# Expert stages of a two-block transformer: 32 slots of 32 rows in four column groups, the two slots of each expert one behind the other

## What is computed

```python
N_EXPERTS, TOP_K, D_EXPERT = 16, 2, 512
def grouped_moe(h, w_router, router_bias, w_gate, w_up, w_down):
    t = h.reshape(-1, D)                          # 256 x 1024
    ...
    combine = (jax.nn.one_hot(eidx, N_EXPERTS, dtype=jnp.float32) * w[..., None]).sum(-2)
    for e in range(N_EXPERTS):
        he = jax.nn.silu(t @ w_gate[e]) * (t @ w_up[e])
        y = y + combine[:, e:e + 1] * (he @ w_down[e]).astype(jnp.float32)
```

## Time and profile before

| | us |
|---|---|
| median of 3 runs | 1887.92 (1886.70 to 1888.09) |
| span of the profiled execution | 1886.8 |
| PE busy | 1814.0 (96%) |
| expert blocks of layer 0 on PE, first gate and up to last down | 308.8 to 586.1 |
| the same, layer 1 | 870.6 to 1135.6 |

### The profile page before, as it was taken

One profiled execution on the slowest core, in us unless ns is written; L12 is line 12 of the kernel. 1 busy time (PEld: TensorE's weight loads), 2 busy tenths in 40 slices (PEclk: granted clock), 3 DMA queues, 4 the chain that ended last, 5 costly groups with the idle time before them and its releaser, 6 DMA issues.

```text
span 1886.8 us, 28242 instructions
## 1 busy us (share of the span) xinstructions
PE 1814.0 (96%) x11785; PEld 1285.6 (68%) x11802; DVE 753.6 (40%) x1282; ACT 663.2 (35%) x1076; POOL 74.5 (4%) x132
## 2 busy tenths in 40 slices
PE   5999999989999999999999999999899999999998
PEld 2888785323335888785333336767699999779998
DVE  4593553000004683553000005213265557656555
ACT  2325441111114335441111112141154556655443
POOL 0000001100001000001100010000000000100000
PEclk8999999999999999999999999999999999999999
DMA  9769955999986665856999957879954543444440
GB/s 377 313 268 374 350 240 236 428 427 428 428 347 273 237 273 226 340 243 245 428 428 427 416 221 288 352 309 415 399 215 182 193 159 112 139 174 179 178 178 22
DMA packets 52755, 540.89 MB, mean 287 GB/s; under 512 B 6768, under 2 KB 11248, under 8 KB 21680
## 3 DMA queue, kind: packets, MB, share of 16 engines
q1 hardware_dynamic: 42800, 505.66, 66.4%
q0 software_dynamic: 9856, 33.82, 4.7%
HBM read 589.53 MB, written 28.84 MB: 328 GB/s over the span
## 4 chain that ended last, share of the span: by engine, by line
PE 80%; DMA 9%; DVE 6%; DVEq 2%; issue 1%; ACT 1%; SPq 0%; ACTq 0%
PE bank L1375 15%; PE bank L995 10%; PE bank L997 10%; PE bank L996 10%; PE bank L1402 7%; PE bank L1045 6%; DMA ring<-in_w_up 5%; PE bank L1054 3%; PE bank L1587 3%; PE bank L1178 2%; PE bank L1506 1%; DMA ring<-in_mlp_w 1%; DMA ring<-in_lru_w_out 1%; PE bank L1353 1%; DVE small L295 1%
## 5 line engine op out<-in xcount | busy, mean ns | idle before, releaser
L995 PE MATMUL bank<-split_x,split_w 128*128 128x256 f32 x896 | 251.3, 280 | 0.8 <-DVE split_w L2828 0.8
L996 PE MATMUL bank<-split_x,split_w 128*128 128x256 f32 x896 | 250.6, 280 | 0.0
L997 PE MATMUL bank<-split_x,split_w 128*128 128x256 f32 x896 | 249.7, 279 | 0.0
L2719 DVE TENSOR_TENSOR hidden<-cqkv,bank 128x256 f32<-128x256 f32 x46 | 19.4, 421 | 515.0 <-ACT cqkv L1947 515.0
L2828 DVE TENSOR_TENSOR split_w<-ring,split_w 128x1024 fp32r<-128x1024 f32 x128 | 156.4, 1225 | 98.0 <-ACT split_w L2074 98.0
L996 PE MATMUL bank<-hx_lo,ring_lo 128*128 128x256 f32 (+1 forms) x656 | 183.6, 280 | 0.0
L995 PEld LDWEIGHTS bank<-split_x,split_w 128*128 128x128 f32 x896 | 168.4, 188 | 1.2 <-DVE split_w L2828 1.2
L996 PEld LDWEIGHTS bank<-split_x,split_w 128*128 128x128 f32 x896 | 168.7, 188 | 0.0
L997 PEld LDWEIGHTS bank<-split_x,split_w 128*128 128x128 f32 x896 | 168.7, 188 | 0.0
L2074 ACT ACTIVATE split_w<-ring 128x1024 fp32r<-128x1024 f32 x128 | 134.4, 1053 | 94.0 <-PE bank L997 87.5
L995 PE MATMUL bank<-hx_hi,ring_lo 128*128 128x256 f32 (+1 forms) x528 | 150.5, 285 | 0.0
(11 more groups left out here) (410 smaller groups left out, 2962.0 us busy)
## 6 DMA issues: line engine op xcount, KB each, us to landing
ring<-in_ada SPq DMA_DIRECT2D x48, 2048.0 KB, 11.5
ring<-in_w_gate SPq DMA_DIRECT2D x32, 2048.0 KB, 13.4
ring<-in_w_up SPq DMA_DIRECT2D x32, 2048.0 KB, 18.5
ring<-in_w_down SPq DMA_DIRECT2D x32, 2048.0 KB, 16.8
ring<-in_mlp_w SPq DMA_DIRECT2D x32, 2048.0 KB, 7.6
ring<-in_w_in SPq DMA_DIRECT2D x16, 2048.0 KB, 11.7
mix<-in_w_gate SPq DMA_DIRECT2D x14, 2048.0 KB, 15.7
mix<-in_w_up SPq DMA_DIRECT2D x14, 2048.0 KB, 20.2
```

Source lines behind the costliest of these rows:

```text
L995: pe.matmul(out, hi, x_hi, start=start, stop=False, **kw)
L996: pe.matmul(out, hi, x_lo, start=False, stop=False, **kw)
L997: return pe.matmul(out, lo, x_hi, start=False, stop=stop, **kw)
```

## The change

Blocks become **slots** of 32 rows. Every expert has 64 own rows in the buffer as before, in two slots that follow each other: slot 2e (`own`, rows 0 to 31) and slot 2e+1 (`flex`, rows 32 to 63). There are no extra blocks. Rows over 64 of an expert go in pieces of 32 rows to the flex slot of an expert that has at most 32 rows (a host; hosts are tried in the order 2, 3, ..., 15, 0, 1). Such a **guest** needs its own weights: SP loads them, under a condition, over the host's weights when the host's own slot is done with them. With the counts above layer 0 has two guests (of experts 6 and 7, in slots 5 and 7) and layer 1 has one (of expert 13, in slot 5).

In a slot the stationary operand has 32 columns, and four matmuls of 256 streamed columns go to four column groups (`32 * g`). The rows of four slots come with four transfers and one set of transposes. Results are stored in four pieces a slot. The last four slots (`KEPT`) are multiplied from SBUF, each as 8 matmuls over 32 rows of the array (`kept_results`).

```diff
-CAP = 64
-XB = (2 * T - 1) // CAP
+ROWS_OF_SLOT = 32
+OWN = 2 * ROWS_OF_SLOT
+SLOTS_OF = [(e, kind) for e in range(NE) for kind in ("own", "flex")]
+GROUPS_BEHIND = {GROUP * (q - 1) + 1: q for q in range(1, NG_ROWS)}
...
                 for n, (e, kind) in enumerate(SLOTS_OF):
+                    then = e if kind == "own" else e + BUFFERS
+                    if then < NE:
+                        which = None
+                        if kind == "own":
+                            i = GUESTS.index(e)
+                            which = (sp.value_load(flex[0:1, i:i + 1], min_val=0, max_val=NE - 1),
+                                     sp.value_load(flex[0:1, NE + i:NE + i + 1], min_val=0, max_val=1))
+                        sp.wait_ge(MP.sem, MP.at(f"gu{n}", l))
+                        load(then, 0, which)
+                        load(then, 1, which)
                     if held:
-                        load(*held)
-                    held = (n, (2,), which)
+                        sp.wait_ge(MP.sem, MP.at(f"d{held[0]}", l))
+                        load(*held[1:])
+                    held = (n, then, 2, which) if then < NE else None
...
                     for k in part:
-                        for g in range(2):
+                        for g in range(4):
                             ins = pe.matmul(
-                                banks[n % 2][CAP * g:CAP * g + CAP, :].rearrange("p (u c) -> p u c", u=2), xT[:, k, :],
-                                gu[:, :, k, 256 * g:256 * g + 256], start=(k == 0), stop=(k == KT - 1))
+                                banks[n % 2][32 * g:32 * g + 32, 0:256].rearrange("p (u c) -> p u c", u=2),
+                                xpT[n // GROUP % 2][:, k, at:at + ROWS_OF_SLOT],
+                                gu[:, :, k, P * g:P * g + P], start=(k == 0), stop=(k == KT - 1))
...
-                        for g in range(2):
-                            at = CAP * (1 - g if n == NB - 1 else g)
-                            ins = pe.matmul(banks[2 + n % 2][at:at + CAP, :],
-                                            hTs[n % 2][:, k % 2, CAP * (k // 2):CAP * (k // 2) + CAP],
-                                            wd[:, k, 512 * g:512 * g + 512], start=(k == 0), stop=(k == 3))
+                        for g in range(4):
+                            ins = pe.matmul(banks[2 + n % 2][32 * g:32 * g + 32, 0:256],
+                                            hTs[n % 2][:, 32 * k:32 * k + 32],
+                                            wd[:, k, 256 * g:256 * g + 256], start=(k == 0), stop=(k == 3))
...
+                def kept_results(n):
+                    pe.wait_ge(MA.sem, MA.at(f"out{n}", l))
+                    i = KEPT.index(n)
+                    for j in range(2):
+                        for g in range(4):
+                            rows_ = slice(32 * g, 32 * g + 32)
+                            ins = pe.matmul(y_of(2 * g + j), outs[n % OUTS][rows_, P * j:P * j + P], shareT[i // 2][rows_, i % 2, :],
+                                            start=(i == 0 and j == 0), stop=True, skip_group_check=True)
                 down(NB - 1)
+                for n in KEPT[:-1]:
+                    kept_results(n)
                 for t in range(TT):
                     earlier_results(t)
-                pe.wait_ge(MA.sem, MA.at(f"out{NB - 1}", l))
-                for k in range(KT):
-                    ins = pe.matmul(y_of(k), outs[k // 4][:, P * (k % 4):P * (k % 4) + P], shareT[:, k // 4, :],
-                                    start=False, stop=True, skip_group_check=True)
+                kept_results(NB - 1)
...
+                flex_at = {e: pool.value_load(flex[0:1, 2 * NE + i:2 * NE + i + 1], min_val=0, max_val=ROWS - ROWS_OF_SLOT)
+                           for i, e in enumerate(GUESTS)}
+                group_rows(1)
...
+                pool.wait_ge(MP.sem, MP.at(f"gu{SLOT_AT[NE - 2, 'flex']}", l))
                 for i in (0, 2, 1, 3):
```

More of the change, by code:

```diff
@@ L86, in _const @@
     for name, n in [("ident", P), ("ones", P), ("freq", 1), ("heads", P), ("turn", DQK), ("pair", 8 * P),
-                    ("future", 2 * P), ("before", P), ("own", NE), ("more", NE), ("extras", XB)]:
+                    ("future", 2 * P), ("before", P), ("own", NE), ("more", NE), ("host", NE), ("host row", NE)]:
         CONST[name] = (at, n)
@@ L382, with loads_before @@
 BUFFERS = 3
[L383 to L408, removed]
+SLOTS_OF = [(e, kind) for e in range(NE) for kind in ("own", "flex")]
+NB = len(SLOTS_OF)
+SLOT_AT = {slot: n for n, slot in enumerate(SLOTS_OF)}
+LOADS = [2 * len(range(i, NE, BUFFERS)) for i in range(BUFFERS)]
+LAST_BLOCK = [SLOT_AT[max(range(i, NE, BUFFERS)), "flex"] for i in range(BUFFERS)]
+GROUP = P // ROWS_OF_SLOT
+NG_ROWS = NB // GROUP
+OUTS = 4
+KEPT = list(range(NB - OUTS, NB))
+FIRST_UNSTORED = min(SLOTS_OF[n][0] for n in KEPT)
+GROUPS_BEHIND = {GROUP * (q - 1) + 1: q for q in range(1, NG_ROWS)}
+RAWS = [len(range(i, NG_ROWS - 1, 3)) for i in range(3)]
+WEIGHTED = [3, 4]
+def loads_before(n):
+    e, kind = SLOTS_OF[n]
+    return 2 * (e // BUFFERS) + 1 + (kind == "flex")
 def moe_steps():
@@ L2308, in places @@
             total = counts[:, TT * NE:(TT + 1) * NE]
-            more, upto, first, below = line(), line(), line(), line()
-            over, base, steps = cols(TT, NE), cols(TT, NE), cols(NE, 3)
-            tt(steps, total.unsqueeze(2).broadcast_to([P, NE, 3]), limits.unsqueeze(1).broadcast_to([P, NE, 3]), ALU.is_gt)
+            more, upto, first, below, spare, rank = line(), line(), line(), line(), line(), line()
+            which, used, guest_row = line(), line(), line()
+            over, base = cols(TT, NE), cols(TT, NE)
+            steps = krs[:, 0:NE * STEPS_OVER].rearrange("p (a b) -> p a b", b=STEPS_OVER)
+            passed = rs[:, 0, 0:NE * NE].rearrange("p (a b) -> p a b", a=NE)
+            tt(steps, total.unsqueeze(2).broadcast_to([P, NE, STEPS_OVER]),
+               limits.unsqueeze(1).broadcast_to([P, NE, STEPS_OVER]), ALU.is_gt)
+            ts(spare[:, 0:NE - 2], total[:, 2:NE], ROWS_OF_SLOT + 0.5, None, ALU.is_lt)
+            ts(spare[:, NE - 2:NE], total[:, 0:2], ROWS_OF_SLOT + 0.5, None, ALU.is_lt)
             wait()
@@ L2336, in places @@
             nc.vector.tensor_reduce(at, both, AX, ALU.add)
+            tt(flex[:, 0:NE], which, const("host"), ALU.add)
+            tt(flex[:, 2 * NE:3 * NE], guest_row, const("host row"), ALU.add)
+            tt(flex_row[:, :], guest_row, const("host row"), ALU.add)
             wait()
@@ L2981, in shape_constants @@
     e = np.arange(NE, dtype=np.float32)
-    put("own", np.tile(CAP * e, (P, 1)))
-    put("more", np.tile(CAP * (NE - 1) - CAP * e, (P, 1)))
-    put("extras", np.tile(np.arange(XB, dtype=np.float32), (P, 1)))
+    put("own", np.tile(OWN * e, (P, 1)))
+    put("more", np.tile(OWN * (NE - 1) - OWN * e, (P, 1)))
+    hosts = np.array(GUESTS, np.float32)
+    put("host", np.tile(hosts, (P, 1)))
+    put("host row", np.tile(OWN * hosts + ROWS_OF_SLOT, (P, 1)))
     return con
```

313 lines of the change are left out of this document (156 added, 157 removed).

## The result

The changed kernel takes 1946.24 us (median of 4 runs, 1941.32 to 1949.38), against 1888.01 us (4 runs, 1886.70 to 1892.45) for the kernel before on the same chip. The ratio is 1.0303, with a 95% interval from 1.0281 to 1.0325. The profiled execution has a span of 1941.7 us, 54.9 us over that of before. The forecast was 1875.

What follows compares the result with a forecast made beforehand. Expert stages have two nearly equal lines, transfers (240 us) and PE (277 us); unchanged transfers limit the gain. -8.1 - 12.7 + 2 x 3.7 = -13.4 us on 1886.8 gives 1873.4 span, median 1.1 over: 1875 us, range 1861 to 1895.

Steps and rivals of the forecast that it cites:

- PE's part: Expert stages: small matmul instructions step at 0.055 us, so a slot takes 5.43 us and an expert 11.5 us.
- the two additions: Before each layer's last `down`: 0.9 us for slower instructions after a wait, 1.5 us for gathers during the last expert's loading.
- The second rival: PE's small-instruction step stays at 0.07 to 0.08 us, a slot takes 7.8 us, in all 1948 us; chance 0.10.
- The volume: Expert stages still load 15 and 14 experts; layer 0's weights, token rows and results take 238 us at 425 GB/s.
- The fourth rival: Transfers lose more through 1 KB stores, four times the requests and longer guest gaps: 1909 us, half of it 1892; chance 0.15.
- The third, gaps at guests: Reason in the rival of slower transfers: the weights' queue has longer gaps at guests than the 9.4 and 7.4 us counted.
- Covered edits: Edits taken as hidden: `shares` some 1.7 us behind slots 3 and 4 each, POOL's four transfers a slot 2.7 us of 8.
- 16.8 us for three guests: Weights' queue empty 9.4 us in layer 0 and 7.4 in layer 1, because requests wait for guests' slots and downs.
- The kept slots: End of each stage: 64 matmuls over 32 array rows at 0.115 us each, 7.4 us, +3.7 in each layer.
- the first rival: Row groups run side by side, and neither slower clock nor gathers cost anything: 1862 us; chance 0.17.
- The new `places` ... +2.0 us: DVE chain from counts to one-hot matrix, ahead of the expert stage: a dozen more operations, +2.0 us, all on the path.

Runs made afterwards that it cites:

- the rows early: Changed kernel, but POOL reads two hosts' row numbers before requesting the first token rows and the other fourteen afterwards: 1927.36 us, ratio 1.0220 to the kernel before.
- the strided kernels: Changed kernel with each of four token-row transfers filling every fourth partition; ratios to the kernel before: 1.0042 (early, from third set), 1.0045 (early, all sets), 1.0180 (late, all sets).

## Why the prediction was wrong

**PE's part was right.** 0.055 us a step, so 5.4 us a slot. The last `down` came 12.1 us behind the last weights (599.4 to 611.5), forecast 12.0 with the two additions. The second rival named 1948 us, near what was measured, but its mechanism is refuted by that step: a right number for a wrong reason, by luck. (The 12 us that it adds besides 28 and 20 have no working either.)

**The volume was right, the rate was not.** "Layer 0: 94.4 + 3.7 + 3.7 MB ... is 238 us at 425 GB/s" took the rate of a kernel whose token rows came over 128 partitions for one with 32. The last byte was forecast 247.5 us after the start of the queue and came after 281.8. The narrow transfers cost 23 us in both layers together (1.0303 against 1.0180, rows late in both), or 33 with the rows early (1.0220 against 1.0045). With rows late and one transfer of 128 from the third set on it is 15 (1.0222); whether the other 8 lie in the first set or in the spread between series of runs is not shown. The fourth rival put 17 us on each layer, where 12 to 17 were found, but of its reasons the runs refute two: with 1 KB stores and four requests a slot all in place, the strided kernels have 425 GB/s and packets of 613 or 614 ns from 443 to 520 us. The third, gaps at guests, holds in cost.

**The failed step.** "Covered edits: ... POOL issues four transfers a slot at 0.53 us each". This counts POOL's transfers and not the 16 reads ahead of them, in front of the first rows that PE needs: 16 x 0.57 = 9.1 of the 13.05 us, the other 3.9 being there with two reads as well. The diff shows the loop of value loads directly ahead of `group_rows(1)`; no number for such a read stood in the sum, and with it no hole of 13 us in each layer's queue. It cost 26 us. The second step that failed is the 425 GB/s of the paragraph above, 23 us.

**Guests.** "The queue runs dry only because expert e+3 can be asked for when the guest's slot is done": the mechanism was right and dips are where they were expected (379, 418 and 438 us, later than forecast by the hole), and their lengths nearly so: 2.1 + 3.5 + 5.2 = 10.8 us in layer 0 and 2.4 + 5.3 = 7.7 in layer 1 with rows early and strided, forecast 9.4 and 7.4. But 16.8 us for three guests were 26, 9 more. A gap costs more than its own length: counted in bytes against 425 GB/s, the first three cost 17.9 us and the other two 12.2.

**Smaller terms.** The kept slots cost 0.3 us more than before (3.96 for 3.62) and not 3.7: four row groups run side by side, as the first rival had it; 7 us of the forecast were too much. "The new `places` ... +2.0 us" was 2.9 in layer 0, read from the last count matmul to the first gate and up (10.3 us before, 13.2 after). The end of the stage has 1.07 us of waiting for ACT behind the kept slots that was not foreseen.

**The balance.** From 1875 to 1946 are 71 us. 26 are the late rows, 23 the narrow transfers, 9 the guests' gaps beyond the forecast, by the runs without guests. 13 more are left: the kernel without late or narrow transfers takes 1896 us where 1875 + 9 = 1884 would be expected. By its trace, the last `down` of layer 0 comes 11.8 us later than forecast, that of layer 1 another 13.0, and the rest of the kernel is 2.6 us faster (a sum of 22, these 9 and 13). Most of it stands in the two queues: from first to last byte they take 259.1 and 239.6 us, forecast 247.5 and 230.6, so 20.6 us more. Of these 13 are the gaps at guests as counted in bytes, 5 are lost at the queues' start and end, and 2 are volume. So the guests' part may be 13 and not 9. None of this remainder was tested by an edit of its own.

## What to carry to other kernels

A transfer that shares its time with a full queue is priced by what it does to the queue's packets, and that goes by the partitions it fills: beside transfers to 32 or 64 neighbouring ones the others took 7 to 36% longer (656 to 834 ns for 614, in the windows from 333 to 346 and from 443 to 520 us), beside 32 in steps of four 613 to 620 ns. Count every instruction ahead of the first request of a stage, reads of numbers into registers above all (0.57 us each on POOL), since one late request can stop the engine whose progress sends the next ones. And read the DMA share beside the GB/s: a low share is a hole and asks who was late, a full share at a low rate asks what else is in flight.

## What the hardware showed

- Token rows over 32 or 64 neighbouring partitions left a full queue (share 1.01) at 392 and 396 GB/s, over every fourth partition at 425.
- A skipped conditional load of 2.10 MB still reads 2.10 MB of memory, without a cost in time that these runs could tell (0 to 5 us, each within its interval).
- One store a slot of 128 partitions x 1 KB, put together to rows of 4 KB, made the kernel 8 us slower than four stores of 32 partitions, with the queue at 417 and not 425 GB/s.
- 64 matmul instructions over four row groups of 32 rows, 256 columns each, pass in some 4.0 us, 0.06 us each.
- A full queue that stood empty for 1.9 to 5.2 us lost 4.3 to 8.3 us of its full rate, counted in bytes.
